# Four weight-block sums of each FFN pair on GpSimd instead of VectorE, with separate semaphores for the activation loads, x in halves and four output banks

## The reference

```
def swiglu(h, w_in, w_out):                 # w_in 2048 x 11264, w_out 5632 x 2048
    a, b = jnp.split(h @ w_in, 2, axis=-1)
    return (jax.nn.silu(a) * b) @ w_out

x = x + gate_mix * mixer_output(...)
x = x + gate_ffn * swiglu(modulate(x, norm_ffn, shift_ffn, scale_ffn), w_ffn_in, w_ffn_out)
return rms_norm(x, norm_f)
```

## Time and profile before

| | us |
|---|---|
| median of 2 runs | 2897.76 (2896.37 to 2899.15) |
| the profiled execution, its own time | 2897.78 |
| its span, first to last instruction | 2896.0 |
| PE busy | 2821.0 (97%) |
| DVE busy | 1939.7 (67%) |
| ACT busy | 970.8 (34%) |
| POOL busy | 272.3 (9%), all but 5 of 474 instructions DMA issues |

### The profile page before, as it was taken

The page is one execution under the profiler, slowest core; times in us unless marked ns, Lnnn a source line. Parts: engine busy times, 40 slices in busy tenths (PEclk is TensorE's granted clock), DMA queues, the critical chain, the costliest instruction groups (busy, mean ns, idle before and its releaser), DMA issues.

```text
span 2896.0 us, 40851 instructions
## 1 busy us (share of the span) xinstructions
PE 2821.0 (97%) x17044; PEld 2454.9 (85%) x17044; DVE 1939.7 (67%) x2657; ACT 970.8 (34%) x1376; POOL 272.3 (9%) x474
## 2 busy tenths in 40 slices
PE   7999999999999999999989999999999999999997
PEld 3688888888888888887879999999999987888886
DVE  6556676985443777887677888888887773333445
ACT  4332333224432522221153443434444342222221
POOL 0002331001233001111000000000000000000000
PEclk9999999999999999999999999999999999999998
DMA  9736974334446437886544444444443335434333
GB/s 408 288 101 150 194 180 133 122 122 129 133 146 199 169 125 275 298 281 244 196 152 149 139 143 148 144 142 140 149 135 117 117 115 187 134 98 138 95 98 111
DMA packets 139387, 473.73 MB, mean 164 GB/s; under 512 B 24401, under 2 KB 24657, under 8 KB 134594
## 3 DMA queue, kind: packets, MB, share of 16 engines
q1 hardware_dynamic: 84226, 302.96, 31.7%
q0 software_dynamic: 47104, 156.09, 16.6%
q10 hardware_dynamic: 7872, 12.06, 1.2%
HBM read 426.53 MB, written 44.43 MB: 163 GB/s over the span
## 4 chain that ended last, share of the span: by engine, by line
PE 88%; DVE 5%; DMA 4%; ACT 2%; issue 1%; POOL 0%; DVEq 0%; SPq 0%; ACTq 0%; POOLq 0%
PE ps L2040 11%; PE ps L2042 11%; PE ps L2041 11%; PE ps L2295 9%; PE ps L2297 9%; PE ps L2296 9%; PE ps L2325 5%; PE ps L2326 5%; PE ps L2327 5%; PE ps L2057 2%; DMA hw_raw<-in_w_in 1%; PE ps L2010 1%; PE ps L2119 1%; PE ps L2058 1%; PE ps L1951 1%
## 5 line engine op out<-in xcount | busy, mean ns | idle before, releaser
L1118 DVE TENSOR_TENSOR hw_lo<-hw_raw,hw_hi 128x1024 fp32r<-128x1024 f32 (+1 forms) x348 | 382.8, 1102 | 641.3 <-ACT hw_hi L678 639.2
L678 ACT ACTIVATE hw_hi<-hw_raw 128x1024 fp32r<-128x1024 f32 (+1 forms) x348 | 334.0, 962 | 1055.4 <-DMA hw_raw<-in_w_in 465.4
L1048 ACT ACTIVATE wx_hi<-wx 128x1024 fp32r<-128x1024 f32 x287 | 303.8, 1059 | 450.0 <-PE ps L2297 431.3
L1765 DVE TENSOR_TENSOR wx_lo<-wx,wx_hi 128x1024 fp32r<-128x1024 f32 x287 | 350.4, 1221 | 59.7 <-ACT wx_hi L1048 59.7
L2295 PE MATMUL ps<-t_hi,wx_hi 128*128 128x256 f32 x1312 | 371.3, 283 | 0.0
L2296 PE MATMUL ps<-t_lo,wx_hi 128*128 128x256 f32 x1312 | 371.3, 283 | 0.0
L2297 PE MATMUL ps<-t_hi,wx_lo 128*128 128x256 f32 x1312 | 371.3, 283 | 0.0
L2040 PE MATMUL ps<-h_hi,hw_hi 128*128 128x512 f32 x896 | 353.7, 395 | 3.2 <-DVE st_b L1383 1.9
L2042 PE MATMUL ps<-h_hi,hw_lo 128*128 128x512 f32 x896 | 350.3, 391 | 0.0
L2041 PE MATMUL ps<-h_lo,hw_hi 128*128 128x512 f32 x896 | 349.6, 390 | 0.0
L2325 PE MATMUL ps<-act_hi,hw_hi 128*128 128x512 f32 x704 | 275.8, 392 | 12.6 <-DVE hw_lo L1118 7.1
(11 more groups left out here) (359 smaller groups left out, 5182.3 us busy)
## 6 DMA issues: line engine op xcount, KB each, us to landing
wx<-in_w_fi SPq DMA_DIRECT2D x164, 512.0 KB, 3.3
hw_raw<-in_w_in SPq DMA_DIRECT2D x128, 512.0 KB, 4.2
ada1m<-in_w_ar POOLq DMA_DIRECT2D x128, 512.0 KB, 4.9
ada_mix<-in_w_ac SPq DMA_DIRECT2D x16, 2048.0 KB, 12.7
hw_raw<-in_w_fo SPq DMA_DIRECT2D x64, 384.0 KB, 3.1
hw_raw<-in_w_fo SPq DMA_DIRECT2D x64, 320.0 KB, 2.9
hw_raw<-in_w_glu SPq DMA_DIRECT2D x32, 512.0 KB, 4.7
hw_raw<-in_w_out SPq DMA_DIRECT2D x32, 512.0 KB, 4.4
```

What stands on the lines that cost most here:

```text
L678: act.activation(hw_hi[slot(n)][:, 0:width(n)], hw_raw[slot(n)][:, 0:width(n)], ACT.Copy).then_inc(w_hi, 1)
L1118: tt(hw_lo[s][:, 0:w], hw_raw[s][:, 0:w], hw_hi[s][:, 0:w].bitcast(F32), SUB).then_inc(w_lo, 1)
L1765: tt(wx_lo[o % 12][:, :], wx[o % 12][:, :], wx_hi[o % 4][:, :].bitcast(F32), SUB).then_inc(w_lo, 1)
```

## The change

1. The four `weight_sum` of a pair move from DVE to POOL. POOL makes `weight_sum(g - 1, 0..3)` behind `store_act(g)` and `ada_in(96 + g)`, for g = 1 to 41. `operand_lo` of operands 0 and 1 of a pair, which overwrites a raw block that the sums read, gets a wait for sum 2 and sum 3.
2. On ACT the high parts of the four h sums are no longer made in one go ahead of `split_hi(N_HU + 8)`, but with a weight split between them.
3. Each of the three loads of a group of activations has a semaphore of its own; `act_hi` waits for the load with its tile alone. For q = 0 the split of the first weight unit comes behind eight tiles, on ACT and DVE.
4. x comes back in two halves of 2 MB with a semaphore each, issued ahead of the last `store_act` and not behind it.
5. The down product rotates over four PSUM banks.

```diff
-    xs_out, xs_in = tf_in
-    act_in, act_st = x0_in, uh_in
+    xs_out, xs_in = tf_in[0], [tf_in[1], tg_in[1]]
+    act_in, act_st = [x0_in[0], x0_in[1], tg_in[0]], uh_in
...
-            def load_act(q, k0, k1):
+            def load_act(q, c):
+                k0, k1 = 4 * c, min(4 * c + 4, QTILES)
                 pool.dma_start(a_raw[q % 2][k0 // ST][:, k0 % ST:k0 % ST + k1 - k0, :],
-                               act_d[:, QTILES * q + k0:QTILES * q + k1, :]).then_inc(act_in[q % 2], 16)
+                               act_d[:, QTILES * q + k0:QTILES * q + k1, :]).then_inc(act_in[c], 16)
+            def weight_sum(p, e):
+                if e == 0:
+                    pool.wait_ge(w_ld[2], 16 * (w_loads[2] + p + 1))
+                    pool.wait_ge(w_ld[3], 16 * (w_loads[3] + p + 1))
+                    pool.wait_ge(w_used, x_free(7 * p + 4))
+                    pool.tensor_tensor(operand(p, 4), operand(p, 3), operand(p, 2), ADD).then_inc(x_sum, 1)
+                if e == 1:
+                    pool.wait_ge(w_ld[0], 16 * (w_loads[0] + p + 1))
+                    pool.wait_ge(x_sum, 4 * p + 5)
+                    pool.tensor_tensor(operand(p, 3), operand(p, 0), operand(p, 3), SUB).then_inc(x_sum, 1)
+                if e == 2:
+                    pool.wait_ge(w_used, x_free(7 * p + 5))
+                    pool.tensor_tensor(operand(p, 5), operand(p, 4), operand(p, 0), SUB).then_inc(x_sum, 1)
+                if e == 3:
+                    pool.wait_ge(w_ld[1], 16 * (w_loads[1] + p + 1))
+                    pool.wait_ge(w_used, x_free(7 * p + 6))
+                    pool.wait_ge(x_sum, 4 * p + 7)
+                    pool.tensor_tensor(operand(p, 6), operand(p, 1), operand(p, 5), SUB).then_inc(x_sum, 1)
             for g in range(TILES - 1):
                 store_act(g)
                 if 2 <= g < 32:
                     ada_in(N_WIDE + g)
+                if 1 <= g <= N_PAIR:
+                    for e in range(4):
+                        weight_sum(g - 1, e)
...
+            pool.wait_ge(w_used, N_D)
+            for half in range(2):
+                pool.dma_start(xout[:, 8 * half:8 * half + 8, :], xs_d[:, 8 * half:8 * half + 8, :]).then_inc(xs_in[half], 16)
             store_act(TILES - 1)
-            pool.wait_ge(w_used, N_D)
-            pool.dma_start(xout[:, :, :], xs_d).then_inc(xs_in, 16)
...
             def act_hi(q, k):
-                act.wait_ge(act_in[q % 2], 16 + 48 * (q // 2 + 1))
+                act.wait_ge(act_in[k // 4], 32 + 16 * q)
...
-            for c in range(4):
-                h_sums_hi(c)
+            h_sums_hi(0)
             split_hi(N_HU + 8)
+            h_sums_hi(1)
             split_hi(N_HU + 9)
+            h_sums_hi(2)
             ffn_silu(1)
             split_hi(N_HU + 10)
+            h_sums_hi(3)
             split_hi(N_HU + 11)
...
-            for k in range(QTILES):
+            for k in range(ST):
                 act_hi(0, k)
             split_hi(N_D)
+            for k in range(ST, QTILES):
+                act_hi(0, k)
             split_hi(N_D + 1)
...
             def operand_lo(o):
                 dve.wait_ge(w_hi, N_W + o + 1)
+                if o % 7 < 2:
+                    dve.wait_ge(x_sum, 4 * (o // 7) + 7 + o % 7)
...
-                elif m == 0:
-                    dve.wait_ge(xs_in, 32)
-                stt(xout[:, m, :], ps[m % 2][:, :], mod_x[:, 5 * KT + m:5 * KT + m + 1], xout[:, m, :],
+                elif m % 8 == 0:
+                    dve.wait_ge(xs_in[m // 8], 32)
+                stt(xout[:, m, :], ps[m % 4][:, :], mod_x[:, 5 * KT + m:5 * KT + m + 1], xout[:, m, :],
...
-            for e in range(4):
-                weight_sum(0, e)
...
-                if p + 1 < N_PAIR and j >= 3:
-                    weight_sum(p + 1, j - 3)
...
-            for k in range(QTILES):
+            for k in range(ST):
                 act_lo(0, k)
             split_lo(N_D)
+            for k in range(ST, QTILES):
+                act_lo(0, k)
...
-                    n, out = N_D + 2 * KT * q + 2 * m, ps[m % 2][:, :]
-                    if KT * q + m >= 2:
-                        pe.wait_ge(fd_free, KT * q + m - 1)
+                    n, out = N_D + 2 * KT * q + 2 * m, ps[m % 4][:, :]
+                    if KT * q + m >= 4:
+                        pe.wait_ge(fd_free, KT * q + m - 3)
```

More of the change, by code:

```diff
@@ L299, in block_kernel @@
     uh_in, x0_in, tf_in, tg_in = ([sem(f"{n}{j}") for j in range(2)] for n in ("uh_loaded_or_act_stored", "x0_loaded_or_act_loaded",
-        "tf_loaded_or_xacc_moved", "tg_loaded"))
+        "tf_loaded_or_xacc_moved", "tg_loaded_or_act_or_xacc_loaded"))
     tb_hi, tb_lo = sem("table_hi_ready"), sem("table_lo_ready")
@@ L646, in store_act, with operand @@
                 pool.dma_start(act_d[:, g, :], f_t[g % 2][:, :]).then_inc(act_st[g % 2], 16)
-            def load_act(q, k0, k1):
+            def load_act(q, c):
+                k0, k1 = 4 * c, min(4 * c + 4, QTILES)
                 pool.dma_start(a_raw[q % 2][k0 // ST][:, k0 % ST:k0 % ST + k1 - k0, :],
-                               act_d[:, QTILES * q + k0:QTILES * q + k1, :]).then_inc(act_in[q % 2], 16)
+                               act_d[:, QTILES * q + k0:QTILES * q + k1, :]).then_inc(act_in[c], 16)
+            def operand(p, j):
+                return wx[(7 * p + j) % 12][:, :]
+            def weight_sum(p, e):
[16 more added lines that the diff above has]
+                    pool.tensor_tensor(operand(p, 6), operand(p, 1), operand(p, 5), SUB).then_inc(x_sum, 1)
             for g in range(TILES - 1):
@@ L656, in _ @@
                     ada_in(N_WIDE + g)
+                if 1 <= g <= N_PAIR:
+                    for e in range(4):
+                        weight_sum(g - 1, e)
             for b in range(2):
                 pool.wait_ge(act_st[b], 16 * 22)
-            for k in range(3):
-                pool.wait_ge(w_used, N_D - 6 + k)
-                load_act(0, 4 * k, min(4 * k + 4, QTILES))
+            for c in range(3):
+                pool.wait_ge(w_used, N_D - 6 + c)
+                load_act(0, c)
+            pool.wait_ge(w_used, N_D)
+            for half in range(2):
+                pool.dma_start(xout[:, 8 * half:8 * half + 8, :], xs_d[:, 8 * half:8 * half + 8, :]).then_inc(xs_in[half], 16)
             store_act(TILES - 1)
-            pool.wait_ge(w_used, N_D)
-            pool.dma_start(xout[:, :, :], xs_d).then_inc(xs_in, 16)
             for b in range(2):
@@ L669, in _ @@
                     pool.wait_ge(w_used, N_D + 2 * KT * (q - 1))
-                for k in range(3):
-                    load_act(q, 4 * k, min(4 * k + 4, QTILES))
+                for c in range(3):
+                    load_act(q, c)
         @block.scalar
```

## The result

The changed kernel takes 2938.9 us (2935.59 to 2942.22, 2 runs) where the kernel before takes 2897.76: ratio 1.0134, interval 1.0106 to 1.0162. It is 41 us slower. The forecast of 2879 was on the wrong side; rival A, priced at 2931, names what happened.

The account below looks back on a forecast made before the run. PE, busy 97% of the span, was taken to bound the kernel. Wins of 4.3 + 9.0 + 6 = 19 us, with the sums on POOL costing nothing, took 2897.8 us to a forecast of 2879, range 2873 to 2960.

Parts of the forecast that it names:

- rival A: Pairs: POOL's sums and DVE's subtractions hold each other up, loop 21.7 us, 2931 us in all; chance 0.37.
- The frame: FFN: at most 21.2 us to win; a gain over 2% (58 us, about what a measurement can tell) impossible, such a loss possible.
- Edit 2: Plain tiles: a weight split between the h sums' high parts removes PE's hole, winning all 4.3 us.
- Edit 3: Boundary behind the pairs: eight tiles suffice if loads land in order, PE goes on without a hole, winning 9.0 us.
- rival C: Boundary: loads land together (2 us, not 9) and x delays weight units as before (3, not 6): 2888 us; chance 0.08.
- Edits 4 and 5: Down product: early x and four banks win between 3 and 7.9 us at the fifth weight unit, taken as 6.
- Edit 1: Pairs: moving the sums to POOL wins nothing, as PE has no hole there, and costs nothing.
- loop 19.3 us, 0.8 us of slack, cost nothing: Pairs: the closed loop through DVE and POOL, 10.5 + 4 s, stays below PE's 20.13 us.
- s: Time of one sum on POOL, bounded by 0.95 and 2.65 us and put at 2.2 us.
- 12.9 + 4 s: Pairs: the loop with two low parts of 1.2 us each added because they cannot run beside POOL's sums; 21.7 us.
- the marks named for A: Pairs: low parts of 2 us or more, stretched sums, PE waiting once or twice a pair, pairs of 21 to 22 us, clock below 1.00.
- The last mark: Pairs as a whole: the forecast is wrong if they take longer than 41 x 20.13 us.

Follow-up runs that it names:

- e1: The changed kernel with the four sums of a pair back on DVE, the other edits kept: 2885.6 us, ratio 0.9949.
- e9: e1 with x issued behind the last store of an activation, as before, still in halves: down product 479.9 us, one execution.
- e5: e1 with the down product over two PSUM banks as before: down product 483.5 us, one execution.
- e3: The changed kernel with the pair operands' low parts taking their second input from PSUM, wrong in value: 2888.1 us, ratio 0.9951.
- e7: The changed kernel with sum 3 back on DVE, sums 0 to 2 on POOL: 2897.8 us, ratio 0.9990.
- e8: The changed kernel with sums 2 and 3 back on DVE, sums 0 and 1 on POOL: 2884.6 us, ratio 0.9938.
- e4: The changed kernel with the four sums ahead of the activation store in POOL's queue: 3039.2 us, ratio 1.0483.

## Why the prediction was wrong

*The frame* held: 21.2 us could be won at most, and a change in the pairs could lose more than that. It was too coarse in one thing: a measurement of this kernel tells far less than 2% from no change. The ratio here is known to 0.3% either way, e1's to 0.13%.

*Edit 2*: all 4.3 us of the plain tiles were won, as worked out.

*Edit 3*: worked out as 9.0, with the loads landing in order. They did, and already in the kernel before (at 2371.4, 2374.0 and 2376.8 us), so the half of rival C that lets them land together does not hold. In e1 the first four high parts start 5.2 us behind the issue and the next four 2.7 us later, and the gap is 1.0 us where it was 8.4. The gap does not hold all of it: the kernel before makes 32 matmuls from 2385.1 to 2394 us, at a granted clock of 0.77 behind the hole, where 39 go in, and most of these 1.7 us stand in its 487.3. In the changed kernel only 4.4 us came in the gap, because its late pairs shortened the time between the last store and the end of the pairs.

*Edits 4 and 5*: 6 us forecast; the down product is 6.4 us shorter in e1 and 8.3 in the changed kernel, a microsecond or so of it edit 3's, as just said. The size was about right, the mechanism wrong: I gave it to the early issue of x; by e9 the hole goes without it once edit 3 is in, and by e5 0.7 us are shown for the banks.

*Edit 1* is the step that failed: "loop 19.3 us, 0.8 us of slack, cost nothing". Two terms of it were wrong. s was put at 2.2 us and is 2.41 without a collision; alone this would have left the loop at 20.1 and cost nothing, as e3 shows. The estimate of 2.25, half of the figure in the Trainium skill (GPSIMD Engine Reference, section 3.1), was 6 to 7% low. The second term decided: the two low parts that fall among the sums were put at nothing, as if they ran beside them. They exclude each other, and rival A's form, 12.9 + 4 s, gives 22.5 at s = 2.4, against 21.92 measured; the 0.6 us too much are its first term (2.14 us, not 2.3) and the two collisions, which cost 0.8 and 1.0 us, not 1.2 each. That A's price of 2931 came within 8 us of 2938.9 is in part luck: with its own form and s = 2.4 it is 2897.8 - 19 + 30 x 2.4 + 10 x 1.2 = 2963, and the s that was too small made up for collisions that were too dear. A was held for 0.37 against 0.45 for the forecast. What should have tipped it is that the loop had less slack than its least certain terms, and that the rule of the Trainium skill that rival A cites described just this pair of instructions, while no row spoke for their running side by side: the absence of such a row was counted as evidence against A, and it was none. The range (2873 to 2960) held the time; the sign was wrong.

*What would show it*: the marks named for A were all there but one: low parts up to 3.44 us, sums stretched to 3.2 and 3.4, PE waiting once or twice in a pair, pairs of 21.9 us. The granted clock did not fall below 1.00 behind these holes of at most 1.5 us. The last mark, pairs longer than 41 x 20.13 = 825 us, could not tell anything: by the reading of the table the kernel before itself takes 829.8, its products 20.16 us apart and with two steps of 1.8 us between matmuls, which e1 and the others have too.

*What stays open*: why the stages ahead of the FFN differ by up to 16 us between executions (the FFN starts between 1470.2, e7, and 1486.1, e9); what edits 4 and 5 would be worth without edit 3; what the banks are worth beyond 0.7 us; and why the clock fell behind a hole of 1.8 us in e3 and not behind one of 2.4 in e1. The version to keep is e1 or e8: both beat the kernel before by 0.5 to 0.6%, and they cannot be told apart.

## What to carry to other kernels

Moving work to an idle engine wins only if the old engine was in the way, and it adds waits: write down the closed loop that passes through both queues and compare its length with the bound's period before counting the work as hidden. GpSimd and VectorE instructions that both read two SBUF blocks run one after the other, so add the VectorE work that falls among GpSimd's to the loop; give VectorE one input from PSUM (timed here only in kernels that leave the right value out), or keep steps of the loop on it (one of four took 38 of 55 us away, two all), and the loss goes. A hole that opens behind a big transfer may be cured by whatever comes earlier: test each edit of a bundle with the others in place.

## What the runs showed of the hardware

- A GpSimd float32 add of 128x1024 takes 2.41 to 2.43 us in the mean when no VectorE instruction with two SBUF inputs meets it (e3), 1.97 times VectorE's 1.22.
- Meeting a VectorE instruction with two SBUF inputs, the one that starts later waits for the whole of the earlier: sums of 3.2 to 3.4 us, low parts up to 3.44, a scalar_tensor_tensor of 1.28 us at 3.43, a product of 0.68 at 2.89. With its second input in PSUM the same VectorE instruction (1.217 us) and the sum (2.41) don't notice each other.
- The profile counts the blocked time as busy; a group whose mean differs between lines of one shape is the sign of it.
- Holes of PE of up to 1.5 us, 64 times, left the granted clock at 1.00; e4, with holes of up to 3.8 us, ran its pairs at 0.91 to 0.95 up to 2400 us. The length of one hole does not decide: in the down product a hole of 1.8 us (e3) and one of 2.3 (e7) were followed by a spell at the lower clock (0.86 and 0.88 over 5 us), one of 2.4 (e1) was not (1.00).
- A load of 384 KB asked for 0.4 us behind one of 4 MB took 13.7 us to land, 4.3 us behind it (in two halves) 11.4 us, and 3.0 us ahead of it 3.1 us.
